# One core, hybrid decoder block with expert retrieval: contiguous x rows beside the masks, and one-hot products in groups of four

## The reference, cut to what matters

```python
h = x + hybrid_mixer(rmsnorm(x), ...)            # 512 tokens x 1024 channels
xn = rmsnorm(h)
q = (xn @ w_query).reshape(t, 8, 2, 128)         # 8 heads, two half queries
scores = einsum('thpk,hpnk->thpn', q, sub_keys)  # 128 keys a half
v1, i1 = top_k(scores[:, :, 0], 16); v2, i2 = top_k(scores[:, :, 1], 16)
best, pos = top_k((v1[..., :, None] + v2[..., None, :]).reshape(t, 8, 256), 16)
e1 = take(i1, pos // 16); e2 = take(i2, pos % 16)
experts = e1 * 128 + e2                          # 128 (head, rank) pairs a token
gates = softmax(best)
a = gelu(sum_d xn[t, d] * expert_u[experts][t, e, d]) * gates
out = rmsnorm(h + sum_e a[t, e] * expert_v[experts][t, e, :])
```

## Time and profile before

| | |
|---|---|
| median of 3 runs | 1597.27 us |
| the profiled execution, its own time | 1597.16 us |
| its span, first to last instruction | 1595.4 us |
| PE busy | 1587.8 us |
| DVE, ACT, POOL busy | 1289.7, 701.6, 426.2 us |
| DMA queues q1, q0, q10 (share of 16 engines) | 39.4%, 28.5%, 9.3% |

### The profile page before, as it was taken

One profiled execution on the slowest core, in us unless ns is written; L12 is line 12 of the kernel. 1 busy time (PEld: TensorE's weight loads), 2 busy tenths in 40 slices (PEclk: granted clock), 3 DMA queues, 4 the chain that ended last, 5 costly groups with the idle time before them and its releaser, 6 DMA issues.

```text
span 1595.4 us, 25473 instructions
## 1 busy us (share of the span) xinstructions
PE 1587.8 (100%) x8590; PEld 1403.7 (88%) x8590; DVE 1289.7 (81%) x2373; ACT 701.6 (44%) x936; POOL 426.2 (27%) x373
## 2 busy tenths in 40 slices
PE   9999999999999999999999999999999999999998
PEld 8888888888888999999999999998888888888886
DVE  6967833334578888988999998779998999999997
ACT  5444533333333433335776776443334333333334
POOL 1011100000000112203353322434445555455451
PEclk9999999999999999999999999999999999999999
DMA  5477632323322699968999999999999999999994
GB/s 214 143 250 239 234 106 96 101 92 100 111 82 78 231 337 318 325 205 281 333 386 410 406 389 379 407 356 373 390 413 387 413 414 394 410 407 397 404 358 162
DMA packets 150237, 459.85 MB, mean 288 GB/s; under 512 B 16336, under 2 KB 47104, under 8 KB 148512
## 3 DMA queue, kind: packets, MB, share of 16 engines
q1 hardware_dynamic: 82080, 231.08, 39.4%
q0 software_dynamic: 47888, 172.15, 28.5%
q10 hardware_dynamic: 20208, 55.94, 9.3%
HBM read 402.78 MB, written 56.33 MB: 288 GB/s over the span
## 4 chain that ended last, share of the span: by engine, by line
PE 98%; ACT 1%; DVE 1%; DMA 1%; issue 0%; SPq 0%; DVEq 0%; ACTq 0%
PE bank L1036 20%; PE bank L1038 20%; PE bank L1037 20%; PE bank L1223 11%; PE bank L1224 11%; PE bank L1222 11%; PE bank L1199 3%; PE bank L1102 1%; DMA h_t<-x_t 1%; PE bank L1236 0%; ACT w_hi L689 0%; DVE w_lo L1275 0%; PE bank L1081 0%; PE bank L1083 0%; PE bank L1082 0%
## 5 line engine op out<-in xcount | busy, mean ns | idle before, releaser
L689 ACT ACTIVATE w_hi<-w_raw 128x1024 fp32r<-128x1024 f32 x347 | 365.9, 1056 | 349.9 <-PE bank L1224 238.9
L1036 PE MATMUL bank<-xn_hi,w_hi 128*128 128x352 f32 (+1 forms) x1472 | 510.4, 347 | 0.0
L1275 DVE TENSOR_TENSOR w_lo<-w_raw,w_hi 128x1024 fp32r<-128x1024 f32 x329 | 401.6, 1221 | 130.8 <-ACT w_hi L689 126.9
L1037 PE MATMUL bank<-xn_lo,w_hi 128*128 128x352 f32 (+1 forms) x1472 | 504.7, 343 | 0.0
L1038 PE MATMUL bank<-xn_hi,w_lo 128*128 128x352 f32 (+1 forms) x1472 | 504.7, 343 | 0.0
L597 POOL DMA_INDIRECT rows<-u_rows,expert x128 | 152.8, 1193 | 610.3 <-DVE expert L1703 353.9
L1222 PE MATMUL bank<-w_hi,a_hi 128*128 128x512 f32 x768 | 298.8, 389 | 0.0
L1224 PE MATMUL bank<-w_hi,a_lo 128*128 128x512 f32 x768 | 298.8, 389 | 0.0
L1223 PE MATMUL bank<-w_lo,a_hi 128*128 128x512 f32 x768 | 298.8, 389 | 0.0
L1038 PEld LDWEIGHTS bank<-xn_hi,w_lo 128*128 128x128 f32 x1472 | 276.7, 188 | 17.7
L1037 PEld LDWEIGHTS bank<-xn_lo,w_hi 128*128 128x128 f32 x1472 | 276.9, 188 | 17.4 <-issue 0.2
(11 more groups left out here) (239 smaller groups left out, 1486.1 us busy)
## 6 DMA issues: line engine op xcount, KB each, us to landing
w_raw<-u SPq DMA_DIRECT2D x128, 512.0 KB, 6.7
w_raw<-v SPq DMA_DIRECT2D x128, 512.0 KB, 7.1
g_dram<-g_sb ACTq DMA_DIRECT2D x12, 2048.0 KB, 10.9
g_in<-g_dram SPq DMA_DIRECT2D x84, 256.0 KB, 9.0
act_dram<-act_out ACTq DMA_DIRECT2D x54, 352.0 KB, 5.7
act_in<-act_dram SPq DMA_DIRECT2D x54, 352.0 KB, 8.5
w_raw<-gate SPq DMA_DIRECT2D x32, 512.0 KB, 3.3
w_raw<-w_in SPq DMA_DIRECT2D x31, 512.0 KB, 3.8
```

Source lines behind the costliest of these rows:

```text
L689: act.activation(w_hi[:, slot, :], w_raw[:, slot, :], ACT.Copy).then_inc(hi_done, 1)
L1036: pe.matmul(out, hi, x_hi, start=k == 0, stop=False)
L1037: pe.matmul(out, hi, x_lo, start=False, stop=False)
L1275: dve.tensor_tensor(w_lo[:, slot, :], w_raw[:, slot, :], w_hi[:, slot, :].bitcast(F32), ALU.subtract).then_inc(lo_done, 1)
```

## The change

It has two parts. The x rows of the extra tokens move from a strided place over `xn_hi` and `xn_lo` (eight pieces of 512 bytes a partition) to 4 KB a partition behind the first three planes of each mask buffer, where only the last two masks have a fourth plane. A buffer is filled by one DMA for 8 tokens instead of 8 DMAs; the four DMAs are issued at q = 20 and 22 and four rows ahead of row 16 and row 24 of the extra rows. And PE does the four groups of a mask behind every second dense tile, ACT the four copies behind every second tile's gelu and `w_hi`.

```diff
+TILES_PER_MASK = ROUND * SLOTS // MASKS_PER_ROUND
-X_STORED, X_LOADED, X_AT_ONCE = 6, 10, 2
+X_STORED, X_LOADED = 6, (EXTRA_SHOWN + 1, EXTRA_SHOWN + 3)
-        beside_xn = MemoryMap(nc, xn_at)
-        x_extra = [beside_xn(f"x_extra{k}", [P, NB, T])[:, :, 0:GT] for k in range(X_BUFFERS)]
+        x_extra = [MemoryMap(nc, at + 2 * (1 + GATE_PARTS) * MASKED * KEYS)(f"x_extra{k}", [P, D])
+                   for k, at in enumerate(mask_regions)]
-            def load_extra(t):
-                g, at = t // SHARED, t % SHARED * SPREAD
-                pool.dma_start(x_extra[g % X_BUFFERS][at:at + SPREAD],
-                               x_rows_dram[t:t + 1, :].broadcast_to([SPREAD, D])
+            def load_extra(g):
+                pool.dma_start(x_extra[g % X_BUFFERS][:],
+                               x_rows_dram[g * SHARED:(g + 1) * SHARED, :].unsqueeze(1).broadcast_to([SHARED, SPREAD, D])
                                ).then_inc(x_extra_loaded[g % X_BUFFERS], 16)
-                if q == X_LOADED:
+                if q in X_LOADED:
                     pool.wait_ge(x_rows_stored, 16)
-                if q >= X_LOADED and q - X_LOADED < X_BUFFERS * SHARED // X_AT_ONCE:
-                    for k in range(X_AT_ONCE):
-                        load_extra(X_AT_ONCE * (q - X_LOADED) + k)
-                kind, r = u_row(q)
-                if kind and SHARED <= r < EXTRA - SHARED and r % SHARED >= ROW_SLOTS:
-                    for k in range(2):
-                        load_extra((r // SHARED + 1) * SHARED + 2 * (r % SHARED - ROW_SLOTS) + k)
+                    load_extra(X_LOADED.index(q))
+                kind, r = u_row(q + SHARED - ROW_SLOTS)
+                if kind and r % SHARED == 0 and r >= X_BUFFERS * SHARED:
+                    load_extra(r // SHARED)
             def g_round(s, last=False, midway=None, after=1):
                 for b in range(ROUND * SLOTS):
                     gelu_tile(ROUND * s + (ONEHOT_AT + b // SLOTS), b % SLOTS)
-                    for q in (2 * b, 2 * b + 1):
+                    for q in range(2 * (b - 1), 2 * (b + 1)) if b % TILES_PER_MASK == TILES_PER_MASK - 1 else ():
                         copy_g(s, q, ...)
+            def mask_groups(s, n, last_round):
+                pe.wait_ge(masks_ready, MASKS_PER_ROUND * s + (n + 1))
+                for q in range(SLOTS * n, SLOTS * (n + 1)):
+                    pe.wait_ge(g_copied, GROUPS_PER_ROUND * s + (q + 1))
...
                     u_tile(ROUND * s + (ONEHOT_AT + b // SLOTS), b % SLOTS)
-                    for q in (2 * b, 2 * b + 1):
-                        if q % 4 == 0:
-                            pe.wait_ge(masks_ready, MASKS_PER_ROUND * s + (q // 4 + 1))
-                        pe.wait_ge(g_copied, GROUPS_PER_ROUND * s + (q + 1))
...
+                    if b % TILES_PER_MASK == TILES_PER_MASK - 1:
+                        mask_groups(s, b // TILES_PER_MASK, last_round)
```

More of the change, by code:

```diff
@@ L145 @@
 EXTRA_SHOWN = DOTS_TOPK + ROW_SLOTS - 1
-X_STORED, X_LOADED, X_AT_ONCE = 6, 10, 2
-assert EXTRA_SHOWN + 2 < EXTRA_FIRST and EXTRA % MASKED == 0
+X_STORED, X_LOADED = 6, (EXTRA_SHOWN + 1, EXTRA_SHOWN + 3)
+assert EXTRA_SHOWN + 3 < EXTRA_FIRST and EXTRA % MASKED == 0
 KEPT_STEPS = 5
@@ L345, in build @@
         assert small.at <= nc.sbuf_usable_end and small.at >= max(rest.at, after_topk.at)
-        beside_xn = MemoryMap(nc, xn_at)
-        x_extra = [beside_xn(f"x_extra{k}", [P, NB, T])[:, :, 0:GT] for k in range(X_BUFFERS)]
-        assert beside_xn.at <= scratch_at
         assert max(rest.at, after_topk.at) <= nc.sbuf_usable_end and gate_loop.at <= nc.sbuf_usable_end
@@ L370, in build @@
                    for k, at in enumerate(mask_regions)]
+        x_extra = [MemoryMap(nc, at + 2 * (1 + GATE_PARTS) * MASKED * KEYS)(f"x_extra{k}", [P, D])
+                   for k, at in enumerate(mask_regions)]
+        assert 4 * D <= 2 * (EXTRA_PARTS - GATE_PARTS) * MASKED * KEYS
         g_build.at += 2 * (1 + EXTRA_PARTS) * MASKED * KEYS
@@ L1179, in _ @@
             pe.sem_inc(onehots_used, SLOTS)
+            def mask_groups(s, n, last_round):
+                pe.wait_ge(masks_ready, MASKS_PER_ROUND * s + (n + 1))
+                for q in range(SLOTS * n, SLOTS * (n + 1)):
+                    pe.wait_ge(g_copied, GROUPS_PER_ROUND * s + (q + 1))
+                    if last_round and q >= GROUPS_PER_ROUND - SLOTS * MASKS_X:
+                        held, parts = masks_x[q // 4 % 2], EXTRA_PARTS
+                    else:
+                        held, parts = masks[q // 4 % 2], GATE_PARTS
+                    for t in range(TOKENS_PER_GROUP):
+                        pair, lane = divmod(TOKENS_PER_GROUP * (q % 4) + t, 2)
+                        for k in range(parts):
+                            last = pe.matmul(bank[4 + q % SLOTS][:, t * KEYS:(t + 1) * KEYS],
+                                             held[:, 0, pair, :, lane], held[:, 1 + k, pair, :, lane],
+                                             start=k == 0, stop=k == parts - 1)
+                    last.then_inc(onehots_used, 1)
             def onehot_round(s, last_round=False, turning=False):
@@ L1672, in dot_extra @@
                 row = rows[:, slot, :].rearrange("p (j d) -> p j d", d=P)
-                dve.scalar_tensor_tensor(row, row, 1.0, x_extra[r // SHARED % X_BUFFERS], ALU.mult, ALU.mult,
+                dve.scalar_tensor_tensor(row, row, 1.0, x_extra[r // SHARED % X_BUFFERS][:], ALU.mult, ALU.mult,
                                          accum_out=dots_extra[:, r:r + 1]).then_inc(rows_used, 1)
@@ L1680, in u_dots @@
                     if kind and r % SHARED == 0:
-                        dve.wait_ge(x_extra_loaded[r // SHARED % X_BUFFERS], 16 * SHARED * (r // SHARED // X_BUFFERS + 1))
+                        dve.wait_ge(x_extra_loaded[r // SHARED % X_BUFFERS], 16 * (r // SHARED // X_BUFFERS + 1))
                     (dot_extra if kind else dot)(r, q % ROW_SLOTS, q // ROW_SLOTS + 1)
```

## The result

The changed kernel takes 1609.71 us (median of 7 runs, 1603.49 to 1611.55), the kernel before 1597.38 us (7 runs): 1.0072 times as long, 95% interval 1.0061 to 1.0082. It is slower where "same" was forecast (1595.5 us, in a range of 1594.6 to 1597.4). The profiled execution took 1608.69 us.

The account below looks back on a forecast made before the run. PE was taken to bound the kernel, busy 1587.8 of 1595.4 us. 24 fewer trips at 0.07 us save 1.7 us, other engines' effects counted as 0: 1597.2 - 1.7 = 1595.5 us, range 1594.6 to 1597.4.

Parts of the forecast that it names:

- PE's price of a trip: PE going from dense matmuls to a one-hot block and back: 0.07 us each, whatever the block's length.
- Rival two: PE's long blocks lose their pace from the 25th one-hot on, 8.8 us more, 1604.3 us; chance 3%.
- The reuse of banks: PE's waits in the block: copies end 5.5 us behind its start, PE returns at 9.5 us, lead over 5 us.
- ACT's four copies: Copies on ACT end 5.5 us behind the block's start, next gelu due at 5.7; what queues behind is 0 to 0.5 us late.
- The last store of G: Last 2 MB store, which holds u tile 116, begins at 988.1; cost taken 0, at most 0.7 us.
- A mask's first need: In the one-hot stage, a mask's first group comes one dense tile later, widening the 0.85 us lead by 3.84 us.
- the paragraph on the x rows: POOL's x loads: 384 KB more are 2 us for four rows, each gathered three dot products ahead; effect on PE 0.
- the paragraph on masks: DVE's masks for PE: the first was ready 0.85 us before use, the stage's thinnest lead, and the change widens it.
- rival three: End of the u stage: late rows use up DVE's 1.03 us lead; a 3 us late landing gives 1597.5 us; chance 4%.
- 25 us is enough: First x load, at turn 20 (gather issued at 731.28), has time for 512 KB before the dot product at 756.90.
- the 1.7 us: Forecast gain on PE: 24 fewer trips to the one-hots at 0.07 us each.
- the number of matmuls is the same: PE's sum: matmuls stay equal in number while blocks go from 48 to 24, dense ones 0.16 us apart.

Follow-up runs that it names:

- e1: The kernel before with only the grouping changed: four groups behind every second dense tile, x rows loaded as before; 1596.66 us, ratio 0.9994.
- e12: The changed kernel with each x row stored 16 times at turn 6 (2 MB), so each load reads 128 rows of its own; 1600.78 us, ratio 1.0018.
- e6: The changed kernel with its four x loads reading 128 different rows of u, x of the extra tokens left out; 1596.43 us, ratio 0.9992.
- e14: The changed kernel with each x load reading 16 rows of u, each for 8 partitions, x of the extra tokens left out; 1597.32 us, ratio 1.0002.
- e13: The changed kernel with each load's order turned: eight tokens in turn, sixteen times over, so extra tokens' products are of other pairs; 1597.39 us, ratio 0.9999.
- e16: The changed kernel with each x row stored twice and each load reading 16 of these, each for 8 partitions, all work done; 1597.33 us, ratio 1.0002.
- e4: The changed kernel with x loads issued one token at a time, two a turn, as before the change but to the contiguous place; 1596.62 us, ratio 0.9993.
- e7: The changed kernel with four x buffers, all loaded at turns 10 to 16, none in the one-hot stage; 1596.54 us, ratio 0.9995.
- e10: e7 with PE's loop over the first four one-hot rounds written out; 1596.62 us, ratio 0.9996.
- e3: The changed kernel with the first two x loads issued at turns 10 and 12 instead of 20 and 22; 1600.5 us, ratio 1.0013.

## Why the prediction was wrong

**Right.** PE's price of a trip: 24 blocks of 32 and 48, each 0.07 us over its one-hots. Rival two (a long block loses its pace) is false: the block of 32 at 804.95 goes at 57 ns a matmul like the earlier trace rows. The reuse of banks and ACT's four copies are as worked out; timeline of ACT, changed kernel, against the earlier trace rows:

```profile
785.92 0.47 ACT L861 ACTIVATE act_out<-bank 128x352 f32<-128x352 f32 x1 [2.35 <-PE bank L1035]
...
787.23 4.02 ACT L875 ACTIVATE g_sb<-bank 128x512 f32<-128x512 f32 x4
791.67 0.46 ACT L861 ACTIVATE act_out<-bank 128x352 f32<-128x352 f32 x1 [0.42 <-PE bank L1035]
```

The copies end 5.33 us behind the gelu (5.5 forecast), and ACT is idle 0.42 us before the next one. The last store of G is issued at 988.88 in e1 (988.1 forecast, 989.07 before) and the u load behind it at 999.50 (999.60), so nothing comes of it. A mask's first need came one tile later, 760.65 in e1 against 756.69.

**The step that failed** is the paragraph on the x rows. It costed the 384 KB that each load adds at 2 us, at the rate of the store of G, and then bounded the effect on PE "by 0 from both sides", since PE had no wait in that stage and its thinnest lead grew. Both halves are wrong.
- *The size.* The rate of a store with up to 16 packets in flight was taken for a load that, as the runs show, has 8 in flight and u loads beside it. No run times the 2 us themselves; three rows together were 10.6 us late, not 2 each with a lead of three dot products in front. (A gather waits for the dot product four turns back, not three as said of the kernel before: extra row 4 is gathered at 767.88, when the dot product of row 0 from 765.85 is done. So three stand between.) With the same 512 KB from an outermost 16 or 128, DVE waits 2.7 us (e12), 4.1 (e6), 6.7 (e14) or 6.9 (e13, e16) for rows between 738 and 762, and PE's waits for masks come to 0 to 1.6 us.
- *The bound.* This is the step that turned a late row into nothing. That PE doesn't wait shows that its lead isn't used up, not how large it is. The lead was read in the paragraph on masks, 0.85 us, and is 4.7 with the change: a bound from the trace would have been "a delay of DVE by more than 4.7 us costs PE the rest". The row lands late, DVE takes its instructions in order, the mask stands behind the row: this chain was missing, though rival three is the same mechanism at the seam.
- *The queue.* "25 us is enough" asked only when x is needed. It didn't ask what the load stands in front of: two gathers and the index load, and POOL then waits 7.19 us.
- *The clock.* A wait was priced at its own length. With both waits the clock fell, and 3.3 us came on top of 8.7.

**The size of the gain** was off as well: of the 1.7 us, 0.9 went to dense matmuls that stand 0.85 ns further apart. The step "the number of matmuls is the same", times a distance taken as fixed, hid that. The kernels with no work left out and no x load of the changed form in the stage (e1, e4, e7, e10) give 1596.5 to 1596.7 us, 0.04 to 0.07% less than before, with intervals that include no change. That is all that the grouping is worth, and contiguous x rows are worth nothing that these runs can tell. e16, the changed kernel with a 16 x 8 load, is at 1597.33 us no faster than the kernel before.

## What to carry to other kernels

For a DMA that is made larger or moved, look at the outermost dimension of both access patterns as well as at the size of a row: a load of 8 x 16 rows of 4 KB had 8 packets in flight and cost 11 to 12 us, one of 16 x 8 had up to 16 and cost nothing clear of noise. Cost it by what stands behind it in its queue and on its engines, followed down to the bottleneck (row, dot product, mask, matmul), and set against the smallest lead on that way; no wait now is no bound of the cost. When an experiment changes a suspected cause, list what else it changes: three runs here fitted repeated rows, and a pair that separated the two properties showed it was the other one.

## What the runs showed of the hardware

- A DMA from a source of 8 x 16 rows had 8 packets of 4 KB in flight, and the stretch 732 to 742 moved 263 to 270 GB/s at a DMA share of 1.03 to 1.04; 16 x 8 rows gave 340 to 347, 128 in one piece 361. From 741 to 742 it was 193 GB/s against 387.
- Beside it the 4 KB packets of other queues took 307 ns instead of 206 on average. The cause isn't shown; the estimate above would give it. Open is why 16 x 8 rows cost 0.9 us more than 128 rows in one piece (1597.3 against 1596.4; whether it is the repeated row or the shape wasn't separated).
- PE's granted clock was 0.50 from 850 to 855 in e3, behind a wait of 3.1 us, and 1.00 in e13 around a wait of 1.1 us (845 to 850):

```profile
845.00:850.00 5.00, 3.92 (x35) 3.63 (x34) 4.48 (x5) 2.24 (x4) 1.14 (x1) 1.00 1.00 408
```

- Dense matmuls of 352 columns have two paces at the full clock, 160.0 and 161.1 ns. With 16 one-hots behind each tile they kept the first, with 32 behind every second mostly the second. In e12, 600 of them without one-hots took 96.67 us (161.1 ns each) from 625.29 on, behind a PE wait at 605. What moves them from one to the other is open.
